# A hybrid decoder layer on eight cores: three small reorderings in the first own tile, and the write-backs of four weight pieces in other tiles

## The reference, cut to what matters

```python
h = rmsnorm(x, g_mix)
q, k, v, u, qm = split(h @ w_in)              # 512, 512, 512, 256, 256 columns
y_attn = three dilated causal windows (128,1), (512,4), (2048,16) with ALiBi, 8 heads,
         merged by their softmax denominators
y_pool = (trailing means over 2, 4, 8, 16 tokens - u) @ w_pool * pool_scale
y_mem  = softmax(qm @ km.T / 8) @ vm           # 256 memory tokens, 4 heads
x = x + concat(y_attn, y_pool, y_mem) @ w_out
h2 = rmsnorm(x, g_ffn)
x = x + relu(h2 @ w_ff1)**2 @ w_ff2            # 1024 -> 4096 -> 1024
return rmsnorm(x, g_final)
```

## Time and profile before

| | us |
|---|---|
| median of 3 runs | 1560.46 (1559.82 to 1602.95) |
| the profiled execution's own time | 1560.62 |
| its span, slowest core (core 6) | 1559.6 |
| spans of the eight cores | 1547.4 to 1559.6 |
| PE busy on core 6 | 1504.7, 96% |
| DVE, ACT, POOL busy on core 6 | 939.6, 748.3, 143.2 |
| HBM read and written | 283.55 MB and 46.92 MB |

### The profile page before, as it was taken

The page is one execution under the profiler, slowest core; times in us unless marked ns, Lnnn a source line. Parts: engine busy times, 40 slices in busy tenths (PEclk is TensorE's granted clock), DMA queues, the critical chain, the costliest instruction groups (busy, mean ns, idle before and its releaser), DMA issues.

```text
span 1559.6 us, 28054 instructions; the slowest of 8 cores (1547.4 to 1559.6 us)
## 1 busy us (share of the span) xinstructions
PE 1504.7 (96%) x9578; PEld 759.5 (49%) x9743; DVE 939.6 (60%) x1427; ACT 748.3 (48%) x1146; POOL 143.2 (9%) x198
## 2 busy tenths in 40 slices
PE   7989989999999999999999999999999999999997
PEld 3445535544554445554455445554455444554446
DVE  4686566664665647655566647556466555556665
ACT  6658664534544354542645335443536335444125
POOL 2011110101101110001000010001000000100001
PEclk9999999999999999999999999999999999999999
DMA  9798698758869568777557583346635383433642
GB/s 287 202 281 219 137 184 153 148 152 282 164 166 208 171 232 188 180 194 234 185 162 202 171 290 117 145 146 214 230 109 184 114 257 110 174 128 133 212 172 74
DMA packets 47418, 285.04 MB, mean 183 GB/s; under 512 B 6192, under 2 KB 11440, under 8 KB 15920
## 3 DMA queue, kind: packets, MB, share of 16 engines
q1 hardware_dynamic: 30480, 179.34, 33.8%
q0 software_dynamic: 15504, 103.62, 29.1%
q10 hardware_dynamic: 1296, 0.29, 0.1%
HBM read 283.55 MB, written 46.92 MB: 212 GB/s over the span
## 4 chain that ended last, share of the span: by engine, by line
PE 86%; DMA 6%; issue 3%; DVE 2%; ACT 2%; ACTq 0%; DVEq 0%; POOL 0%; SPq 0%; POOLq 0%
PE mm L406 73%; PE ob L804 7%; PE sc L779 4%; DMA ring<-wall 3%; DMA wscratch<-ring 1%; DMA colr<-acc 1%; PE sc L672 1%; DMA X<-xh 1%; DVE acc L437 0%; ACT P L427 0%; PE sc L406 0%; PE mm L1135 0%; ACT Vd L568 0%; ACT sq L427 0%; DVE X L1013 0%
## 5 line engine op out<-in xcount | busy, mean ns | idle before, releaser
L406 PE MATMUL mm<-aT,ring 128*128 128x512 bf16 (+2 forms) x2150 | 453.4, 361 | 16.9 <-DMA ring<-wall 6.7
L406 PE MATMUL mm<-h2T,ring 128*128 128x512 bf16 x1980 | 458.5, 379 | 9.6 <-issue 8.3
L781 ACT ACTIVATE P<-sc 128x1024 bf16<-128x1024 f32 x256 | 247.7, 1021 | 190.8 <-PE sc L779 189.8
L406 PEld LDWEIGHTS mm<-aT,ring 128*128 128x128 bf16 x2208 | 201.6, 98 | 213.8 <-issue 16.2
L406 PEld LDWEIGHTS mm<-h2T,ring 128*128 128x128 bf16 x2048 | 191.2, 98 | 222.9 <-issue 12.8
L786 DVE TENSOR_TENSOR P<-P,E 128x1024 bf16<-128x1024 bf16 x224 | 156.1, 701 | 190.7 <-ACT P L781 190.7
L950 ACT ACTIVATE rt<-mm 128x512 f32<-128x512 f32 x226 | 134.8, 596 | 212.6 <-PE mm L406 168.4
L963 DVE TENSOR_TENSOR aT<-rt 128x512 bf16<-128x512 f32 x224 | 161.7, 736 | 72.4 <-ACT rt L950 70.4
L427 ACT ACTIVATE sq<-X 128x512 f32<-128x512 f32 (+2 forms) x196 | 118.3, 610 | 137.3 <-DVE X L992 86.9
L406 PE MATMUL mm<-hT,ring 128*128 128x512 bf16 x659 | 146.3, 379 | 0.9 <-ACT P L950 0.2
L804 PEld LDWEIGHTS ob<-P,Vd 128*128 128x128 bf16 x1664 | 112.7, 98 | 52.3 <-issue 4.4
(11 more groups left out here) (143 smaller groups left out, 1036.7 us busy)
## 6 DMA issues: line engine op xcount, KB each, us to landing
ring<-wscratch SPq DMA_DIRECT2D x125, 1024.0 KB, 5.9
ring<-wall POOLq DMA_DIRECT2D x43, 1024.0 KB, 10.2
wscratch<-ring SPq DMA_DIRECT2D x21, 1024.0 KB, 6.0
X<-xr POOLq DMA_DIRECT2D x16, 1024.0 KB, 11.5
out<-X POOLq DMA_DIRECT2D x14, 1024.0 KB, 10.4
X<-xh POOLq DMA_DIRECT2D x12, 1024.0 KB, 15.0
X<-xh SPq DMA_DIRECT2D x6, 1024.0 KB, 16.1
vscratch<-Vd POOLq DMA_DIRECT2D x24, 192.0 KB, 8.1
```

The costliest lines, as they stand in the source:

```text
L406: T.op("pe", lambda: nc.tensor.matmul(out_ap, lhsT=l, rhs=r, start=(i == 0), stop=(i == n - 1)), reads=rd, writes=[b_out], mark=(i == n - 1))
L781: T.op("act", lambda: nc.scalar.activation(out=P_[:], in_=s_[:], func=AF.Exp, scale=0.125), reads=[bs_], writes=[bP_])
```

## The change

Four edits. (a) `turn`: FF1_1 is written back in own tile 2 instead of 0, FF1_2 in own tile 3 instead of 0, FF2_4 in own tile 0 instead of 3, FF2_6 in own tile 0 instead of 2. So FF1_1 is cast in tiles 1 and 2 and FF1_2 in tiles 1, 2 and 3, where both came from the scratch; FF2_4 in tiles 1 to 3 and FF2_6 in tiles 1 and 2 come from the scratch, where they were cast. Each tile keeps its four MLP write-backs, and casts and scratch loads over the whole run are as many as before. (b) In the first own tile's projections the norm sum of the memory tokens goes from position 4 to 5 and that of the next tile from 13 to 15, with the products behind each. (c) In `att_over`, where a batch with `post` is the first of its step (10 and 24), `back` of the second is held until `front` of the next batch has been issued. (d) In its last step the final product runs on DVE instead of POOL.

```diff
-                        [0, 0, 0, 1, 2, 3, 1, 2, 0, 3, 1, 2, 3, 1, 2, 3]))
+                        [0, 2, 3, 1, 2, 3, 1, 2, 0, 3, 1, 2, 0, 1, 0, 3]))
...
-        def back(bt):
+        def back(bt, e="pool"):
...
-            T.op("pool", lambda: nc.gpsimd.tensor_tensor(out=yT[:, ch, :], in0=val[:], in1=den[:], op=ALU.mult),
+            T.op(e, lambda: (nc.vector if e == "dve" else nc.gpsimd).tensor_tensor(out=yT[:, ch, :], in0=val[:], in1=den[:],
+                                                                                  op=ALU.mult),
...
+            kept = []
             for i in range(0, n + 2, 2):
                 for b in bts[i:i + 2]:
                     front(b)
                     out += 1
+                    while kept:
+                        back(kept.pop())
...
                 if i >= 2:
-                    for b in bts[i - 2:i]:
-                        back(b)
-                        if b["post"] is not None:
-                            fill(2)
+                    a, b = bts[i - 2:i]
+                    back(a)
+                    if a["post"] is not None:
+                        fill(2)
+                        if i < n and b["post"] is None:
+                            kept.append(b)
+                            continue
+                    back(b, "dve" if i == n else "pool")
+                    if b["post"] is not None:
+                        fill(2)
...
-        side += ln_side(mln, 0, 0.3, 4, 4.2, 0.3)
+        side += ln_side(mln, 0, 0.3, 5, 5.2, 0.3)
         if two:
-            side += ln_side(lns[j + 1], 7, 0.5, 13, 13.4, 0.6)
+            side += ln_side(lns[j + 1], 7, 0.5, 15, 15.3, 0.5)
```

## The result

Forecast were 1553 us with a range of 1544 to 1561. Measured were 1568.34 us (median of 6 runs, 1564.94 to 1569.94) against 1560.15 us for the kernel before on the same chip: a ratio of 1.0054 [1.0044, 1.0064]. The change makes the kernel 8 us slower, outside the range on the slow side.

What follows compares the result with a forecast made beforehand. TensorE was busy 96% of the span, so only its waits and lowered clock could change. Core 0, then slowest, summed to 1555.1 - 7.0 + 4.3 = 1552.4, plus 1.0 for execution over span: 1553 us, range 1544 to 1561.

Steps and rivals of the forecast that it cites:

- Edit (a), later tiles: MLP start in tiles 1 and 2: new casts just in time, +0.5 us each; end of tile 1: -1.9 or -2.1.
- Rival D: Tiles 1 and 2: FF1_1's cast waits behind both input loads, 7.3 and 8.6 us plus clock; 1570 us; chance 0.10.
- Edit (b): First own tile's two norm sums: waits shrink by 1.05 and 2.0 us, clock loss behind them by 1.7 (core 6).
- The clock at 100 to 110: Around the norm-sum wait, core 6 granted 0.83: 1.7 us lost, taken as gone with the wait.
- Edits (c) and (d): Waits on `val` at batches 10 and 24 shrink by 0.6 us, the wait for POOL's last product by 0.3.
- The next product of the norm: Eight products of the next tile's norm arrive in time or 0.3 us late; cost taken at nothing.
- The end of the first MLP: Near 318 us, added write-backs delay FF2_6 by 3.9 us: PE waits 2.9 on core 6, 3.3 on core 0.
- Rival C: The wait near 318 us also lowers the clock, 3.4 us more: 1557 us, or 1559 with FF2_7; chance 0.13.
- The start of the first MLP: Core 6 near 218 us: FF2_0's wait of 4.8 us goes, with 3.4 us of clock loss; none on core 0.
- The end of tile 1: Wait for FF2_6 goes as it comes from scratch on SP: -1.9 us on core 6, -2.1 on core 0.
- The clock of core 0 from 180 to 220: Granted 0.93 with PE busy: 2.8 us lost to a die-wide limiter, which no edit removes.

Runs made afterwards that it cites:

- e3: The whole change with the `X<-xh` loads emitted at position 18.9 instead of 23.4, ahead of the casts of FF1_1 and FF1_2; 1553.41 us, ratio 0.9969.
- e1: The whole change without its new write-back table: edits (b), (c) and (d) with the old table; 1552.57 us, ratio 0.9964.
- e12: Edits (c) and (d) alone on the kernel before, with the old table and old norm positions; 1557.96 us, ratio 0.9991.
- e5: Edits (b) to (d), inputs at 18.9, old table with FF1_1's write-back moved to tile 1 and FF2_2's to tile 0; 1563.16 us, ratio 1.0012.
- e9: Like e5, with the write-backs of FF1_2, FF1_6 and FF2_5 moved as well; 1561.85 us, ratio 1.0026.
- e2: The kernel before with the new write-back table alone, without edits (b) to (d); 1569.57 us, ratio 1.0076.
- e10: The whole change with ACT's squares of the late-loaded tile from MLP group 11.2 instead of 6.2; 1557.68 us, ratio 0.9987.

## Why the prediction was wrong

**The step that failed** is "Edit (a), later tiles", in its sentence that FF1_1 and FF1_2 "become casts behind the two `X<-xh` loads". I took the order from the times of issue in the old trace: the input at 368.2, FF1_1 at 371.3. But these were on two queues, POOL's and SP's. Once FF1_1 is a cast it is issued by POOL, at its place in POOL's own order of emission. `load_x` has position 23.4, after FF1_1's issue (end of group 19) and FF1_2's (end of group 23), so the casts go first, and POOL waits in front of each until PE frees the buffer. The inputs, which nobody waited for before, then go out 13.5 us later against PE and behind two casts. I priced the casts (+0.5 for each of two tiles) and never asked what the move does to what comes after them. The old trace had the consumer too, the square on ACT. Rival D had the right sign, queue, tiles and nearly the right total (1570), but with the roles reversed; in e3 its own order costs at most 1.0 us, perhaps 1.6, in a tile, where it forecast 7.3 and 8.6. That its total came near is luck. With the failed step taken out the rest of the forecast would have stood: e3 is at 0.9969, or 1555 us against the 1560.15 of the first comparison, inside the range of 1544 to 1561, though not for all of its reasons: the terms below that were too small and too large partly cancel.

**Terms that held.** Edit (b): the waits of 1.05 and 2.44 us went, and 0.39 and 0.40 us came for evacuations of PSUM, one behind the first sum and one between the two. With the clock the sum gave 1.05 + 2.0 + 1.7 = 4.7 us; e1 against e12 gives 4.2 (2 to 6.5). The clock at 100 to 110 came to 1.00 on core 6 too, where the earlier trace rows have 0.83. Edits (c) and (d): -0.9 forecast, 0.0009 x 1559 = 1.4 us measured (0 to 2.8). The next product of the norm was not late.

**The end of the first MLP.** Forecast were 3.3 us on core 0 and 2.9 on core 6; measured were 3.09 near 310 and 1.01. Core 0 is the only one of the forecast cores 0, 3 and 6 in the forecast 2 to 4 us, core 3 has 0.55, and cores 2 and 4 have no wait. The mechanism was right (FF2_6 late beside a write-back), but the size was not the full 3.9 us: on core 6 its cast took 17.7 us against 15.7 in the earlier trace rows, so 2.0 were added, of which 1.0 was margin. That core 0 hit the number is partly luck. Rival C's mechanism came with it, since this wait drew a fall of the clock on core 0, but of 1.5 us, not 3.4.

**The start of the first MLP.** The 4.8 us of wait were rightly explained: FF2_0 is issued on PE's release, and there is no wait near 218. The clock behind them was mis-sized: of the 10 x 0.21 + 10 x 0.13 = 3.4 us, the part in which PE was still idle costs nothing, and the six busy microseconds from 226.85 were granted 0.52, which is 2.9 us. And the term did not turn into gain. e1 keeps the old table, is at 0.9964, and has waits of up to 3.54 us there; e3 has the new table with its harm removed and is at 0.9969. The intervals overlap: taking two write-backs away at 196 to 215 buys no more than the waits near 307 (2.3 us on core 2 of e3) and at the end of tile 1 (3.1 us) give back.

**The end of tile 1** was to lose its wait of 1.9 to 2.1 us for FF2_6. It became 2.97 us on core 0, for the same piece from the scratch. SP's timeline:

```profile
480.48 0.32 SPq L100 DMA_DIRECT2D wscratch<-ring  x1
480.95 14.40 SPq L100 DMA_DIRECT2D ring<-wscratch  x2
```

PE was through with the buffer at 477.9, but the write-back of FF2_5 waits on SP for its cast until 480.45, and the load of FF2_6 goes out behind it, 3.1 us late. It then takes 17.2 us, as long as the cast that it replaced (17.1). I counted half the bytes and not the queue into which the load moved. It is the same mistake as the first, on another queue, and e5 and e9 repeat it at 8.5 and 5.3 us.

**The clock of core 0 from 180 to 220** was held to be outside the reach of any edit. All four cores of the first die had 0.92 or 0.93 there in the kernel before, and all four of the second 1.00. After the change, and also in e1, e2, e3 and e12, all eight cores have 1.00, and e12 has the old table and the old norms. So it came and went with the execution and not with an edit. The Trainium skill ("TensorE: Matmul & The Clock Gate", section "Seeing it yourself") has a limit that takes a whole die once three of its cores run dense matmuls. The trace agrees in that all four cores of one die had it. But all cores were as busy in these five profiles as before, and the clock stayed up, so that condition alone does not bring it on here; what does, no run shows. What was wrong was to leave the 2.8 us in a sum for the next kernel.

**Not settled.** How the 9 us between a first input load of 20.4 and of 11.1 us split between the casts, the load of `Vd` ahead of it in the same queue and the write-back beside them was not separated. Why e10, with no long wait for `rt`, seems to stay some 3 us above e3 (0.9987 against 0.9969; the intervals overlap) is only partly named by its rows (2.3 for the scratch load, 2.1 for `P`).

The best version is e1, edits (b) to (d) with the old table: 0.9964 [0.9952, 0.9976], some 5.6 us. e3 can't be told from it.

## What to carry to other kernels

When a transfer changes its queue, don't compare times of issue from the old trace: walk through the order in which the code emits for the new queue, and list what now stands behind the transfer, including what had so much margin that no view named it. Then ask of each such transfer which in-order engine consumes it and what that engine owes to the bottleneck. And before a wait of a single profiled core goes into a sum, look for it on the other cores and in a second profile: here one wait was 0 to 5.6 us, and one fall of the clock belonged to the execution.

## What the runs showed of the hardware

A write-back whose issue waits for a landing held a ready load on the same queue: the load went out 0.5 us behind it, then took 16.0 us (e5, core 0), against 12.2 us for the same kind of load of FF1_1 in the earlier trace rows. The same 1 MB input load took 7.9 us with no cast ahead of it, 11.1 on a queue of its own beside the casts, and 20.4 behind two casts. Around the waits of 5.9 to 8.7 us for `rt` every core was at 1.2 GHz for 6.8 to 10.2 us. Part of that fell into the wait and cost nothing; the 2.8 to 5.8 us of it in which PE was busy again cost another 1.4 to 2.9 us.
